# A mixture-of-experts decoder trunk: the last down unit of a layer split into two column halves, each copied and combined by itself

## What is computed

```
gates = top-1 group, then top-2 experts inside it, weights renormalised
hg = jnp.einsum('btd,edf->btef', x, w_gate)
hu = jnp.einsum('btd,edf->btef', x, w_up)
h = jax.nn.silu(hg) * hu * gates[..., None]
ffn = jnp.einsum('btef,efd->btd', h, w_down)
x = layer_norm(DEEPNORM_ALPHA * x + ffn, ln_ffn_g[layer], ln_ffn_b[layer])
```

## Time and profile before

| | us |
|---|---|
| median of 3 runs | 1549.71 (1546.44 to 1553.23) |
| profiled execution | 1553.17 |
| its span | 1551.4 |
| TensorE busy | 1374.1 (89%) |
| DMA ring and work units | 430 GB/s at most in one of 40 slices of the span |
| mean granted TensorE clock | 0.966 |

### The profile page before, as it was taken

One profiled execution on the slowest core, in us unless ns is written; L12 is line 12 of the kernel. 1 busy time (PEld: TensorE's weight loads), 2 busy tenths in 40 slices (PEclk: granted clock), 3 DMA queues, 4 the chain that ended last, 5 costly groups with the idle time before them and its releaser, 6 DMA issues.

```text
span 1551.4 us, 18461 instructions
## 1 busy us (share of the span) xinstructions
PE 1374.1 (89%) x7790; PEld 786.1 (51%) x7790; DVE 344.0 (22%) x881; ACT 309.9 (20%) x760; POOL 64.4 (4%) x99
## 2 busy tenths in 40 slices
PE   8999988878999979988789999887789999988875
PEld 7856633332564665533226876332328766633321
DVE  0234311012200982211002034110012143311002
ACT  0233221111211421222112002221110242212110
POOL 2100000000000520000000000000001000000000
PEclk9999899999999989999999999999999999899998
DMA  9754399999743008699999834999997255399996
GB/s 327 268 218 175 124 429 427 429 427 425 299 150 135 42 8 373 267 428 428 427 425 413 349 140 174 417 427 427 428 427 308 110 217 217 144 430 427 428 426 260
DMA packets 35766, 480.74 MB, mean 310 GB/s; under 512 B 4304, under 2 KB 4624, under 8 KB 6368
## 3 DMA queue, kind: packets, MB, share of 16 engines
q1 hardware_dynamic: 34416, 476.92, 74.4%
q0 software_dynamic: 1120, 2.09, 0.7%
q10 hardware_dynamic: 144, 0.48, 0.1%
HBM read 478.36 MB, written 1.05 MB: 309 GB/s over the span
## 4 chain that ended last, share of the span: by engine, by line
PE 64%; DMA 22%; DVE 8%; ACT 3%; issue 2%; SPq 1%; DVEq 0%
DMA ring<-in_units 17%; PE psum L662 15%; PE psum L906 9%; PE psum L676 9%; PE psum L694 7%; PE psum L882 6%; DMA work<-in_units 5%; PE psum L936 5%; PE psum L944 5%; PE psum L684 2%; ACT work L1037 2%; DVE work L1424 1%; PE psum L998 1%; PE psum L627 1%; DVE work L1576 1%
## 5 line engine op out<-in xcount | busy, mean ns | idle before, releaser
L662 PE MATMUL psum<-xT,ring 128*128 128x256 f32 x1024 | 226.5, 384 | 2.8 <-DVE xT L1258 2.2
L662 PEld LDWEIGHTS psum<-xT,ring 128*128 128x128 f32 x1024 | 197.1, 193 | 31.5 <-issue 3.1
L944 PE MATMUL psum<-work 128*128 128x512 f32 x256 | 127.1, 622 | 42.9 <-DVE work L1576 22.8
L882 PE MATMUL psum<-work,x 128*128 128x128 f32 x1024 | 131.4, 283 | 35.6 <-ACT work L1037 35.0
L906 PE MATMUL psum<-ring,work 128*32 128x512 f32 x1200 | 141.6, 605 | 23.5 <-DMA ring<-in_units 23.5
L882 PEld LDWEIGHTS psum<-work,x 128*128 128x128 f32 x1024 | 120.9, 194 | 71.3 <-issue 67.6
L676 PE MATMUL psum<-ring,xT 128*128 128x512 f32 x320 | 138.3, 593 | 0.1
L1037 ACT ACTIVATE work<-psum,affine_t 128x128 f32<-128x128 f32 x256 | 96.4, 457 | 129.6 <-PE psum L882 129.6
L1571 DVE TENSOR_TENSOR work<-work,psum 128x256 f32<-128x256 f32 x32 | 13.5, 421 | 487.1 <-ACT work L1177 487.1
L906 PE MATMUL psum<-work 128*32 128x512 f32 x848 | 104.7, 629 | 17.1 <-DMA work<-in_units 17.1
L694 PE MATMUL psum<-ring,work 128*128 128x512 f32 x256 | 110.6, 593 | 0.5 <-DVE work L1487 0.5
(11 more groups left out here) (197 smaller groups left out, 1144.8 us busy)
## 6 DMA issues: line engine op xcount, KB each, us to landing
ring<-in_units SPq DMA_DIRECT2D x138, 2048.0 KB, 27.0
work<-in_units SPq DMA_DIRECT2D x83, 2048.0 KB, 26.7
ring<-in_units SPq DMA_DIRECT2D x6, 1024.0 KB, 46.2
ring<-in_units SPq DMA_DIRECT2D x4, 512.0 KB, 8.3
work<-in_units SPq DMA_DIRECT2D x2, 1024.0 KB, 46.4
x<-in_x SPq DMA_DIRECT2D x2, 512.0 KB, 4.3
out<-x SPq DMA_DIRECT2D x2, 512.0 KB, 2.6
work<-in_tables SPq DMA_DIRECT2D x1, 768.0 KB, 30.6
```

The costliest lines, as they stand in the source:

```text
L662: last = nc.tensor.matmul(bank(key, T, s * T), w[:, 2 * m + s, k, :], xT[:, k, :], start=(k == 0), stop=(k == KD - 1))
L882: last = nc.tensor.matmul(psum[:, to, i * P:(i + 1) * P], xk, sel[:, par, c, :], start=(c == 0), stop=(c == TC - 1))
L944: last = nc.tensor.matmul(psum[:, 4 + NH * c + h, :], hT[:, FC + c, :], y_sb[:, h * HB:(h + 1) * HB], start=False, stop=last_quad, skip_gr ...
```

## The change

The second down unit of each quad is packed as two column halves (b = 0: columns 512 to 767, b = 1: 768 to 1023), each with both blocks j. In the ordinary quads `down(1)` reads both halves as one matmul of 2 x 256 columns. In the last quad of a layer the order is down(0), combine(0), then for each b: `last_down(b)`, a copy by ACT, `last_combine(b)`. The second half's results go to bank 0. `third_filled` and `third_ready` are the semaphores of b = 0; `unit_used` and `y1_ready` serve b = 1. `combine(0)` is not held back behind `down(1)` any more.

```diff
                 def down(h):
                     pe.wait_ge(*slots[GU + h][1])
-                    w = slots[GU + h][0].rearrange("p (j e c) -> p e j c", e=QE, j=FC)
+                    if h:
+                        w = slots[GU + h][0].rearrange("p (b j e c) -> p e j b c", b=2, e=QE, j=FC)
+                    else:
+                        w = slots[GU + h][0].rearrange("p (j e c) -> p e j c", e=QE, j=FC)
                     for j in range(FC):
-                        if j and h == NH - 1 and last_quad and sems is first:
-
-                            pe.wait_ge(half_in, 16 * (n // NQ + 1))
                         for e in range(QE):
                             rows = slice(W * e, W * (e + 1))
-                            last = nc.tensor.matmul(psum[rows, 2 + h, :], hT[:, j, rows], w[:, e, j],
+                            to = psum[rows, 2 + h, :]
+                            last = nc.tensor.matmul(to.rearrange("p (b c) -> p b c", b=2) if h else to, hT[:, j, rows], w[:, e, j],
                                                     start=(j == 0), stop=(j == FC - 1))
                     last.then_inc(sems["unit_used"], 1)
+
+                def last_down(b):
+
+                    pe.wait_ge(*((half_in, 16 * (n // NQ + 1)) if b else slots[GU + 1][1]))
+                    w = slots[GU + 1][0].rearrange("p (b j e c) -> p b e j c", b=2, e=QE, j=FC)
+                    for j in range(FC):
+                        for e in range(QE):
+                            rows = slice(W * e, W * (e + 1))
+                            last = nc.tensor.matmul(psum[rows, (3, 0)[b], 0:HB // 2], hT[:, j, rows], w[:, b, e, j],
+                                                    start=(j == 0), stop=(j == FC - 1))
+                    last.then_inc(unit_used if b else third_filled, 1)
+
+                def last_combine(b):
+
+                    pe.wait_ge(*((first["y1_ready"], n + (1 + FREE)) if b else (third_ready, n // NQ + 1)))
+                    cols = slice(b * HB // 2, (b + 1) * HB // 2)
+                    for c in range(TC):
+                        last = nc.tensor.matmul(psum[:, 4 + NH * c + 1, cols], hT[:, FC + c, :], y_sb[:, HB:D][:, cols],
+                                                start=False, stop=True, skip_group_check=True)
+                        if b:
+                            last.then_inc(z_ready, 1)
...
-                if last_quad:
+                if last_quad and sems is first:
                     down(0)
-                    down(1)
-                    combine(0)
-                    last = combine(1)
+                    combine(0).then_inc(half_ready, 1)
+                    for b in range(2):
+                        last_down(b)
+                        last_combine(b)
...
+                if last_quad:
+                    act.wait_ge(third_filled, l + 1)
+                    nc.scalar.activation(y_sb[:, HB:HB + HB // 2], psum[:, 3, 0:HB // 2], ACT.Copy).then_inc(third_ready, 1)
                 act.wait_ge(sems["unit_used"], n * QU + (QU + spare(sems)))
-                nc.scalar.activation(y_sb[:, HB:D], psum[:, 3, :], ACT.Copy).then_inc(sems["y1_ready"], 1)
+                if last_quad:
+                    nc.scalar.activation(y_sb[:, HB + HB // 2:D], psum[:, 0, 0:HB // 2], ACT.Copy).then_inc(sems["y1_ready"], 1)
+                else:
+                    nc.scalar.activation(y_sb[:, HB:D], psum[:, 3, :], ACT.Copy).then_inc(sems["y1_ready"], 1)
...
-        moe[:, GU:] = inputs["moe_w_down"][l].reshape(NQ, QE, FC, P, NH, HB).transpose(0, 4, 3, 2, 1, 5).reshape(NQ, NH, P, UNIT)
+        down = inputs["moe_w_down"][l].reshape(NQ, QE, FC, P, NH, 2, HB // 2)
+        moe[:, GU] = down[:, :, :, :, 0].transpose(0, 3, 2, 1, 4, 5).reshape(NQ, P, UNIT)
+        moe[:, GU + 1] = down[:, :, :, :, 1].transpose(0, 3, 4, 2, 1, 5).reshape(NQ, P, UNIT)
```

More of the change, by code:

```diff
@@ L374, in build @@
         unit_used, half_ready = sem("unit_used"), sem("half_ready")
+        third_filled, third_ready = sem("third_filled"), sem("third_ready")
         bank_filled = sem("bank_filled")
@@ L1172, in tokens, with quad @@
                 ins.then_inc(sems["xw_ready"], 1)
-            def quad(l, sems, n, par, ahead):
+            def quad(l, sems, n, par, ahead, last_quad=False):
                 act.wait_ge(sems["unit_used"], n * QU + (GU + spare(sems)))
@@ L1191, in experts @@
                 for par in range(2):
-                    quad(l, first, l * NQ + NQ - 2 + par, par, par == 0)
+                    quad(l, first, l * NQ + NQ - 2 + par, par, par == 0, par == 1)
             def experts_more(l, runs):
```

## The result

The change makes the kernel slower by 1.46%: ratio to the kernel before 1.0146, 95% interval 1.0122 to 1.017. The medians are 1570.49 us (6 runs, 1565.09 to 1571.63) and 1548.08 us (6 runs, 1539.41 to 1553.23). The prediction was 1552.8, its range ended at 1560, and it gave slower 7 in 100. It was wrong.

The account below looks back on a forecast made before the run. The prediction took each layer's end to be bound by the last down half's transfer, replaced by PE's own queue. Four ends (-1.2, +0.9, +2.1, +0.5) plus 0.8 for the clock gave +3.1 on 1549.71: 1552.8 us, range 1546 to 1560.

Parts of the forecast that it names:

- The tail, step by step: End of each expert phase: a serial chain on PE and its copiers, 7.63 us from S to DVE's second-half statistics.
- S: Start of DVE's copy of the first down result in a layer's last quad, as down(0) ends; the tail's starting mark.
- The sum: Four layer ends plus clock: -1.2 + 0.9 + 2.1 + 0.5 + 0.8 = +3.1 us, giving 1552.8.
- the -1.2 of layer 0: End of layer 0: second-half statistics at 380.27 instead of 381.48, so 1.2 us won.
- The +0.8 for the clock in layer 1: Layer 1's tail: half clock falls on 1.5 us of the new combine(0) and costs half of it, 0.8 us.
- What costs nothing, and what hides it: Part listing free or hidden work: moved statistics, table load hidden with 0.25 us to spare, later slot release, two-piece reads zero.
- the ten extra matmuls a layer (20 records) are in the chain above: PE's layer ends: the added matmuls cost only their time already counted in the 7.63 us chain.
- Won or lost there goes to the total one to one: Tail into next mixer: the mixer starts from the tail's end, so any shift reaches the total fully, four times.
- B: Rival: PE's clock falls in the longer tail; four whole layers give +22, 1572 us; chance 0.08.
- C: Rival: other phases swallow the shift, as experts' transfers run at their own rate; time stays 1549.7; chance 0.18.
- A: Rival: the tail is transfer-bound and the split pays, 9.4 us less, 1540; chance 0.06 whole or in part.
- What I listed as the sign of being wrong: In the tails: last_down still starting on the landing, clock near 0.5, or 256-column pass spacing other than 0.216.

Follow-up runs that it names:

- e1: The changed kernel with all TensorE instructions moved 170 slots by an alignment directive, work unchanged: 1549.04 us, ratio 1.0018 to the kernel before.
- e3: Control: the kernel before with the same alignment directive, set so that by count nothing moves: 1544.56 us, ratio 1.0005 to the kernel before.
- e2: The kernel before, work unchanged, with its TensorE code moved so that the jump targets lie two blocks on: 1562.88 us, ratio 1.0107.
- e4: The changed kernel without the overflow path on TensorE (no test, no jump, none of its 300 instructions): 1545.67 us, ratio 1.001 to the kernel before.
- e8: e7 plus a branch prefetch hint at the start of each layer's last quad and the test as an explicit branch: 1552.01 us, ratio 1.0031.
- e5: The changed kernel, moved as in e1, with PE's last-quad order down(0), last_down(0), combine(0), last_down(1), last_combine(0), last_combine(1): 1539.68 us, ratio 0.9958 to before.
- e7: The changed kernel with its TensorE code moved to another place (offset 51), no hint: 1569.21 us, ratio 1.0145 to the kernel before.

## Why the prediction was wrong

- **The tail, step by step: right.** Its 7.63 us from S were 7.60, 7.60 and 7.68 in three layers after, and 7.61, 7.61, 7.60 and 7.67 in e1. That PE's own queue takes the place of the wait for the transfer was right, and so were the prices of a combine, a down and a copy of 256 columns (0.38 in every L1204 row seen). Layer 1 took 9.48: its `combine(0)` ran at the lower clock from end to end, 3.78 us for 1.98, which cost 1.9 where I counted 0.8. Layer 0 had no fall, as counted.
- **The sum: near for the edit, wrong for the kernel, and near in part by luck.** Where the position is held (e1), the time is 0.18% over before, 2.8 us of 1549.7, with the interval from nothing to 6; I had said +3.1. But its old tails came from one execution, in which the clock had fallen: 8.84, 6.71, 5.51 and 7.16 us from S. In e3, the same work at the same place, they are 7.19, 5.52, 5.79 and 5.88, so the -1.2 of layer 0 isn't there, and e1's four tails are 6.1 us longer than e3's in sum; its median is 4.5 us over e3's. The +0.8 for the clock in layer 1 isn't in e1 either (7.61).
- **The step that failed** is in "What costs nothing, and what hides it": "the ten extra matmuls a layer (20 records) are in the chain above". I counted them as time on PE alone. They are also 40 instructions of program text, and they push PE's jump over the overflow path, and everything behind it, through the blocks in which code is fetched. The three idle times of 4.09, 6.29 and 5.86 us come from that, and the half clock behind them; e1, e2 and e4 show it from three sides, and the jump itself shows it in the trace, 6.70 and 6.27 us for 0.3. That price had no term, no bound and no rival in the sum, so the range had no place for it.
- **"Won or lost there goes to the total one to one"** was the wrong reading of the same spot: I looked at the next mixer's matmuls in their unbroken run and not at how PE gets from the tail to it. Before, L621 followed the last combine with no idle time, which I took for the rule and not for a matter of place.
- **The rivals.** B, the clock in the tail, was on the right side with the wrong mechanism: one tail of four shows it (and one of e8, 9.47 us in layer 2). Its 1572 is near the measured time by chance. C was wrong as a whole, though some of the loss did come back in the expert phases behind the stops. That those were shorter because the transfers went on is read from the balance; no run tested it. A was wrong for the order of the change, and e5 shows it at work in another order.
- **What I listed as the sign of being wrong** was a fall of the clock or a landing in the way; the "issue" idle time stood in none of the lists.

How much of a stop is the fetch itself? In the ten stops seen (the changed kernel, e2, e7, e8), PE goes on 6.0 to 6.8 us behind the start of the jump; what PE still had to run in that time makes the idle time 2.2 to 6.3. The packet takes 1.0 to 1.2 us of it. In layers 0 to 2 of all the profiled kernels that have the jump, it starts 3.5 to 4.2 us behind the jump, with some 100 to 120 packets of the unit transfers started in between. In layer 3, where all units have landed and no packet of theirs is in between, it starts 1.0 to 1.7 us behind it. By this comparison some 2.5 us of a stop come only beside the unit transfers. That is an estimate from these times; no run held that traffic back.

## What to carry to other kernels

An edit that adds instructions moves all the code behind it. Where an engine's program has a taken jump over some hundred instructions, count jump and target in blocks of 256 instructions before and after, and when a kernel changes by a few microseconds at each jump with no releaser named, move the code without changing it before explaining the edit. Splitting work to fit a late transfer paid here only in the order where something else ran while each piece was copied (e5 against e1): between the matmuls that feed a copy and those that need it, there must be another piece.

## What the runs showed of the hardware that was not expected

- A taken jump of 301 instructions costs TensorE nothing or leaves it idle for 3.7 to 6.3 us ahead of its next matmul, by the place of its code in the blocks alone (e1 and e3 against the changed kernel, e2 and e7). The jump itself takes 0.3 to 0.4 us, or 6.0 to 6.7 where its target isn't fetched.
- The end of a block that isn't followed by a fetched one shows as a stop of its own: PE stops 20 matmuls and weight loads behind the target in e7, and 8 behind it in the changed kernel, whose jump is 10 slots later.
- The 16 KB transfer behind a jump starts after 3.5 to 4.2 us beside the unit transfers, and after 1.0 to 1.7 us without them (layers 0 to 2 against layer 3, nine profiled kernels).
- Work already queued shortens the stop: 4.1 us with 3.70 us of combines queued (e2), 5.6 to 6.3 with 1.13 queued.
- A prefetch hint some 290 instructions ahead of the jump took both stops of over 5 us away and left the one of 2.2 us (e7 to e8, ratio 1.0145 to 1.0031).
